# Third modulation group of the even layer summed by VectorE instead of TensorE, with the row handoff to DRAM issued later

## The reference, cut to what matters

```python
mod = jax.nn.silu(c) @ w_ada[layer] + b_ada[layer]
sh1, sc1, g1, sh2, sc2, g2 = jnp.split(mod[:, None, :], 6, axis=-1)
hcur = rms_norm(x, norm1_g[layer]) * (1 + sc1) + sh1
...                      # layer 0: dilated attention (o_a) and spatial gating (o_b)
mix = jnp.concatenate([o_a, o_b], -1) @ ev_w_out[j]
x = x + g1 * mix
hcur = rms_norm(x, norm2_g[layer]) * (1 + sc2) + sh2
x = x + g2 * hierarchical_moe(hcur, ...)
```

## Time and profile before

| | |
|---|---|
| median of 3 runs | 1177.52 us (1177.3 to 1179.76) |
| the profiled execution's own time | 1178.81 us |
| its span on the core | 1177.1 us |
| TensorE matmuls busy | 1114.5 us (95%) |
| VectorE, ScalarE, GpSimd busy | 414.2, 272.4, 91.5 us |
| bytes moved by DMA | 353.83 MB, 301 GB/s in the mean |
| mean granted TensorE clock | 0.989 of full |

### The profile page before, as it was taken

How to read it: one execution, slowest core, us unless ns; L and a number is a source line. 1 busy time by engine, 2 the same in 40 slices (tenths; PEclk the granted TensorE clock), 3 DMA queues, 4 the chain that set the end, 5 groups by cost and what they waited for, 6 DMA issues and landing times.

```text
span 1177.1 us, 17038 instructions
## 1 busy us (share of the span) xinstructions
PE 1114.5 (95%) x6890; PEld 646.3 (55%) x6891; DVE 414.2 (35%) x1065; ACT 272.4 (23%) x579; POOL 91.5 (8%) x156
## 2 busy tenths in 40 slices
PE   3999989999999999989899999998999999999997
PEld 0756434444444378554344444444886878767883
DVE  0275254112111089943511111114541444341213
ACT  2214332111111031162211111114002555541201
POOL 0300030000000000230000000000010323210000
PEclk9999999999999999999899999998999999999999
DMA  9998899999999987995799999999595455344000
GB/s 363 365 355 344 213 417 376 424 425 429 428 428 428 411 325 297 293 274 181 317 379 425 428 429 429 429 430 387 174 291 176 150 167 174 104 149 155 18 1 36
DMA packets 69380, 353.83 MB, mean 301 GB/s; under 512 B 5540, under 2 KB 7756, under 8 KB 49868
## 3 DMA queue, kind: packets, MB, share of 16 engines
q1 hardware_dynamic: 61656, 340.68, 75.1%
q0 software_dynamic: 6000, 9.17, 2.9%
q10 hardware_dynamic: 1668, 3.21, 0.7%
HBM read 350.84 MB, written 1.15 MB: 299 GB/s over the span
## 4 chain that ended last, share of the span: by engine, by line
PE 77%; DMA 15%; DVE 4%; ACT 2%; issue 2%; ACTq 0%; SPq 0%; DVEq 0%
PE bank L497 29%; PE bank L870 22%; DMA ring<-in_moe_w_up 11%; PE bank L535 8%; PE bank L826 3%; PE bank L891 3%; DMA arena<-in_ev_w_s 2%; DVE arena L1738 2%; DMA ring<-in_ev_w_in 2%; PE bank L550 1%; PE bank L1145 1%; PE bank L521 1%; PE bank L509 1%; PE bank L711 1%; PE bank L726 1%
## 5 line engine op out<-in xcount | busy, mean ns | idle before, releaser
L870 PE MATMUL bank<-ring,arena 128*32 128x512 f32 x3072 | 337.5, 595 | 9.7 <-issue 3.9
L497 PE MATMUL bank<-arena,ring 128*128 128x256 f32 x1536 | 340.0, 382 | 1.9 <-ACT arena L1286 1.7
L497 PEld LDWEIGHTS bank<-arena,ring 128*128 128x128 f32 x1536 | 290.5, 191 | 47.3 <-issue 8.7
L870 PEld LDWEIGHTS bank<-ring,arena 128*32 128x32 f32 x3072 | 102.3, 110 | 231.5 <-issue 229.7
L535 PE MATMUL bank<-ring,arena 128*128 128x512 f32 x288 | 126.0, 593 | 0.0
L535 PEld LDWEIGHTS bank<-ring,arena 128*128 128x128 f32 x288 | 54.2, 190 | 65.2 <-issue 64.8
L2258 DVE TENSOR_TENSOR arena<-arena,bank 128x512 f32<-128x512 f32 x16 | 11.0, 687 | 197.0 <-PE bank L870 197.0
L826 PEld LDWEIGHTS bank<-arena 128*128 128x128 f32 x512 | 58.5, 192 | 12.0 <-issue 11.7
L826 PE MATMUL bank<-arena 128*128 128x128 f32 x512 | 61.2, 278 | 0.0
L1464 ACT ACTIVATE arena<-bank 128x512 f32<-128x512 f32 x16 | 9.6, 597 | 210.5 <-PE bank L870 210.5
L891 PE MATMUL bank<-arena 128*128 128x512 f32 x128 | 57.7, 594 | 0.0
(11 more groups left out here) (327 smaller groups left out, 900.6 us busy)
## 6 DMA issues: line engine op xcount, KB each, us to landing
ring<-in_moe_w_gate SPq DMA_DIRECT2D x32, 2048.0 KB, 14.7
ring<-in_moe_w_up SPq DMA_DIRECT2D x32, 2048.0 KB, 17.2
ring<-in_moe_w_down SPq DMA_DIRECT2D x32, 2048.0 KB, 13.0
ring<-in_w_ada SPq DMA_DIRECT2D x24, 2048.0 KB, 21.7
ring<-in_w_in SPq DMA_DIRECT2D x16, 2048.0 KB, 11.2
ring<-in_w_c SPq DMA_DIRECT2D x6, 2048.0 KB, 32.8
ring<-in_ev_w_in SPq DMA_DIRECT2D x5, 2048.0 KB, 14.5
ring<-in_od_w_in SPq DMA_DIRECT2D x5, 2048.0 KB, 15.5
```

The lines of the kernel that those rows point to most:

```text
L497: mm = pe.matmul(ps[k0][:, t * S:(t + 1) * S], w[:, k, c:c + P], rhs[:, k, :], start=(k == 0), stop=(k == KT - 1))
L870: mm = pe.matmul(bank[col:col + CHUNK, :], lhs[:, k, col:col + CHUNK], ring[:, (s0 + e) % RING, cut], start=start, stop=stop, tile_positio ...
```

## The change

Units `ada8` to `ada11` move from TensorE's `group_main` to VectorE's `modulate`: `modulate(8)` stands between `score_max` and `score_probs` of head 4, `modulate(9)`, `(10)` and `(11)` behind `gating()`. Because the sum buffer is reused, the first unit of a later group waits until TensorE has summed the group before. `group_whole(2, 11)` stands between `evo0` and `evo1`, the columns between the two halves of `evo1`. On VectorE `group_cols(2)` and `gain(1)` move behind the two additions of `evo0`; on ScalarE the gate's diagonals (`early_diagonals("gateB")`) move ahead of the third square. On GpSimd's queue the bias table now comes first, behind a wait for the third group's `group_whole`, and `affine_by_row(0)` behind `rpb_sent`. The rest is renamed semaphores: `group_whole` is one counter, and six of the router's become `routing_sums_full` and `routed`.

```diff
-SUMMED = (4, 5, 6, 7, 16, 17, 18, 19, 28, 29)
-SUMMED_GROUPS = (1, 4)
+SUMMED = (4, 5, 6, 7, 8, 9, 10, 11, 16, 17, 18, 19, 28, 29)
+SUMMED_GROUPS = (1, 2, 4)
...
                     if n < 2:
                         quarter_by_channel("ev3", hT, n + 2)
-                    else:
-                        group_main(2, (0, 1))
                 elif n == 0:
                     mix()
-                    group_main(2, (2,))
-                elif n == 1:
-                    group_main(2, (3,))
-                else:
-                    group_columns(2)
...
             by_token("evo0", oT, arrived=heads_out)
-            by_token("evo1", oT, arrived=first_tile(1))
+            group_whole(2, 11)
+            by_token("evo1", oT, lambda: group_columns(2), arrived=first_tile(1))
...
-                if p == 3:
-                    group_copy(2)
                 dilated_out(p)
...
             act.wait_ge(sem("gmlp_ready"), 2)
-            early_diagonals("gateB")
-            routed_norm(1)
+            group_copy(2)
+            routed_norm(1, lambda: early_diagonals("gateB"))
...
+                if n % 4 == 0 and n > 4:
+                    dve.wait_ge(sem("group_whole"), SUMMED_GROUPS.index(n // 4))
...
                 score_max("dilated")
+                if h == 4:
+                    modulate(8)
                 score_probs("dilated")
             gating()
-            group_cols(2)
-            gain(1)
+            for n in (9, 10, 11):
+                modulate(n)
...
                 for b in range(TT):
                     add_mixed(names[0], 0, b, tmp)
+                behind_first()
...
+            def second_group():
+                group_cols(2)
+                gain(1)
+
+            routed_norm(1, ("evo0", "evo1"), second_group)
...
             broadcast_gate(0, mod[:, 16:24])
-            affine_by_row(0)
-            pool.wait_ge(sem("ada_ready"), 12)
+            pool.wait_ge(sem("group_whole"), 2)
             step(pool.memset(rpb_pad[0:16, :, :], 0.0))
...
             pool.wait_ge(sem("rpb_sent"), 16)
+            affine_by_row(0)
```

More of the change, by code:

```diff
@@ L562, in group_whole @@
                                    part[:, 512 * g:512 * g + 512], start=True, stop=True, tile_position=(0, 32 * g))
-                mm.then_inc(sem(f"group_{group}_whole"), 1)
+                mm.then_inc(sem("group_whole"), 1)
             one_of_32 = ident.rearrange("p (g r) -> p r g", r=32)[:, 0, :]
@@ L1350, in group_copy @@
                 if group in SUMMED_GROUPS:
-                    act.wait_ge(sem(f"group_{group}_whole"), 1)
+                    act.wait_ge(sem("group_whole"), SUMMED_GROUPS.index(group) + 1)
                 else:
@@ L1545, in _, with routed_norm @@
                     both("ev3", uT, ACT.Gelu_apprx_tanh)
-            def routed_norm(r):
+            def routed_norm(r, ahead=lambda: None):
                 no = r - 1
@@ L1551, in routed_norm @@
                 for n, (t, h) in enumerate(((0, 0), (1, 0), (0, 1))):
+                    if n == 2:
+                        ahead()
                     act.wait_ge(sem("x_half"), 4 * no + n + 1)
@@ L2082, in route @@
                 lg = rt[:, 0:40].rearrange("p (t c) -> p t c", c=20)
[L2083 to L2085 removed]
+                dve.wait_ge(sem("routing_sums_full"), 3 * layer + 1)
+                dve.tensor_copy(logit_parts, ps[4][:, 0:S]).then_inc(sem("routed"), 1)
+                dve.wait_ge(sem("routing_sums_full"), 3 * layer + 2)
                 dve.wait_ge(sem("rw_loaded"), 16 * 7 * (layer + 1))
@@ L2200, in route @@
                 step(dve.tensor_tensor(by_tile(within), by_tile(rank), slots_bc, ALU.is_le))
-                dve.tensor_tensor(by_tile(over), by_tile(rank), slots_bc, ALU.is_gt).then_inc(sem("over_ready"), 1)
+                dve.tensor_tensor(by_tile(over), by_tile(rank), slots_bc, ALU.is_gt).then_inc(sem("routed"), 1)
                 step.wait()
@@ L2204, in route @@
                 step.wait()
-                dve.wait_ge(sem("over_ready"), layer + 1)
+                dve.wait_ge(sem("routed"), 4 * layer + 4)
                 return weights
@@ L2462, in _ @@
             dve.wait_ge(sem("gate_rows_loaded"), 16)
-            routed_norm(1, ("evo0", "evo1"))
+            def second_group():
+                group_cols(2)
+                gain(1)
+            routed_norm(1, ("evo0", "evo1"), second_group)
             dve.wait_ge(sem("rpb_sent"), 16)
```

18 lines of the change are left out of this document (9 added, 9 removed).

## The result

The changed kernel takes 1196.55 us in the median (1195.85 to 1196.72, 5 runs), the kernel before 1177.52 us on the same chip (1177.26 to 1184.33, 5 runs). The ratio, worked out over all these runs, is 1.0154, with a 95% interval of 1.012 to 1.0189: slower, clear of the noise, though by less than 2%. Between the medians it is 19.0 us. The forecast was 1195.6 us.

The account below looks back on a forecast made before the run. TensorE (77% of the chain) was taken as the bound, counted at the router's start: 17.15 us late plus 1.0 for the clock, +18.1 on 1178.81 is 1196.9. Less 1.3 to the median: 1195.6 us, range 1185 to 1201.

Parts of the forecast that it names:

- the handoff's 22 us from gain to values: GpSimd's queue carries gains and shifts through DRAM to ScalarE's second norm: 22 us, with 3.5 us to spare.
- TensorE's part: From heads to output projection: 8.3 us of matmuls removed, projection starts at 127.6, only 0.4 us left at its end.
- The unit in the gap: `modulate(8)` at head 4 on VectorE waits for TensorE's sum, runs 101.3 to 104.95; loss rounded to 0.5 us.
- GpSimd's queue: Bias table takes 13.4 us, element writes behind it from 156.1 take 14.7, the read 6.3: values at 177.7.
- Rival (1): GpSimd's table gets through before the gain is ready: router +5.2 to +7.5 us, 1183 to 1190 us; chance 0.20.
- The clock's term: Behind TensorE's stand, turns and router's matmuls may run at half speed: nothing to 3.1 us, taken as 1.0.
- Writes that take longer (2): Element writes on GpSimd's queue take 26.7 us: router +25.5 us, 1204 us, half way 1200; chance 0.10.
- Hidden (3): Gain to ScalarE's values within 9.1 us costs nothing: router 0.4 us earlier, 1177.1 us median; chance 0.05.
- Absorbed by the experts' loop (4): The experts' partly DMA-bound loop catches up a few us of the late start: 1188 to 1193 us; chance 0.03.

Follow-up runs that it names:

- e2: Kernel before, with only the bias table moved ahead of the gains and shifts on GpSimd's queue: 1189.12 us, ratio 1.008.
- e3: Changed kernel, layer 0's second norm taking its gains and shifts in their old order without waiting, their four DRAM transfers still running: 1267.35 us.
- e4: Kernel before, with the same edit as e3 (old order, no wait, transfers still running): 1262.84 us.
- e8: e3 with the four transfers of gains and shifts left out altogether: 1265.08 us, ratio 1.0711.
- e11: Changed kernel, with TensorE putting layer 0's second-norm gains and shifts in their second order, nothing through DRAM for them: 1185.51 us, ratio 1.0073.
- e12: Kernel before, with the same edit as e11 (order made by TensorE, no transfers): 1185.12 us, ratio 1.0061.
- e1: Changed kernel, with gains and shifts put ahead of the bias table again on GpSimd's queue: 1194.85 us, ratio 1.0137.
- e5: Changed kernel, with `modulate(8)` moved from head 4 to behind the gating, so four units follow it: 1205.04 us, ratio 1.0205.
- e6: e1 with the shifts sent early on their own behind the gate row, only the gains written late: 1191.53 us, ratio 1.0087.
- e7: e6 with `modulate(9)` ahead of the gating, and `group_whole`, columns and gain moved earlier: 1183.23 us, ratio 1.0036.
- e9: e7 with the bias table made near the start, in bytes free then: 1184.5 us, ratio 1.0055.

## Why the prediction was right, step by step

*The mechanism held.* The step that decided, the handoff's 22 us from gain to values with 3.5 us to spare, is shown from three sides: made late by itself it costs 9 to 12 us (e2); without its wait the routers of both kernels start within 0.3 us of each other (e3, e4), or 1.7 us with the transfers gone too (e8 against e4); and without it altogether the kernels' times differ by 0.4 us (e11, e12). Two later takings bear out the other half, that ScalarE could take the values as late as 160.1: 14.5 us later moved the router by 12.0 us (e2), 19.7 us later by 17.2 us (the kernel after), so 2.5 us beyond the 3.5 cost nothing.

*TensorE's part.* The forecast left 0.4 us of the 8.3 us removed at the projection's end, at 160.1; it ended at 161.7, 1.2 us later than before. The projection was to start at 127.6 and started at 130.12. Of these 2.5 us, 1.0 was there when `mix` started (124.08; 0.9 of it already at the second group's `group_whole`, 101.09 instead of 100.23). The other 1.5 us come behind that, and they are a term that was missing. The forecast let TensorE wait for ScalarE ahead of `mix`, with nothing left to fill the wait, but took `mix` at its old 1.95 us. It took 3.38, and the turn behind it 0.81 instead of 0.55. Ahead of it TensorE had stood for 1.04 and 1.95 us; in the kernel before it was busy throughout, and the granted clock in this window was 1.00. The window of the kernel after:

```profile
124.00:128.00 4.00, 3.92 (x19) 3.65 (x19) 1.95 (x5) 0.24 (x1) 0.55 (x1) 0.57 0.56 37
```

The unit in the gap was released by TensorE's sum as forecast: VectorE's first pass started at 102.33, after `group_whole` at 101.09. `group_whole` of the third group found its three units summed (no stand at 144.03), as forecast too, and the gain was ready at 153.4 instead of 151.0.

*GpSimd's queue.* The bias table's share was right: 13.4 us forecast from `group_whole`'s end to `rpb_sent`, 13.2 measured from the clearing to the writes. The mis-sized term is the writes: 14.7 us were taken from the earlier trace rows, 11.2 were measured; the read's 6.3 us were 7.1. The start 2.3 us late and the writes 3.5 us short cancel but for the read: values at 177.3 (forecast 177.7), router at 183.22 (forecast 183.2). The agreement of the sum is better than that of its terms, and to that extent it is luck.

*What the argument got wrong without harm.* It laid 5 us of the loss on the table standing ahead of the writes. e1 shows 0.4 us at the router: writes that start earlier ran beside more of the ring's loads and lasted longer. Rival (1), less traffic, was so half right: the writes did get shorter, but the table was not through before the gain. The clock's term was 1.0 us. The turn alone took 0.85 us more (1.94 against 1.09), and from the router's first matmul to the experts 20.28 us passed instead of 17.52, 0.77 of it in the router's matmuls; by the end of the span these 2.8 us are gone again, in stretches that the change does not touch. So 17.0 us stand between the profiled executions, where the forecast had 18.1.

*The other rivals.* Writes that take longer (2): the slower one landed after 10.0 us, not 26.7; e2 shows that the direction was possible (17.5 us for the pair), but not in this place. Hidden (3): the writes of the kernel after never landed in less than 8.4 us, and from gain to values it took 24 us where 9.1 would have cost nothing. The Trainium skill, page DMA: Bandwidth & Descriptors (Anatomy of one DMA — SWDGE (gpsimd) path), gives about 2.0 us of fixed cost. No write of single elements in this case comes near it (8.4 us is the shortest in layer 0), and the measurement decides. Absorbed by the experts' loop (4): 19.93 us late at its first matmuls and 20.03 us behind it, at the second layer's first turn, so it absorbed nothing.

*What the trace of before could not show.* The element writes take something from the ring's loads when these are the experts' first weights (e3 against e8: 2.3 us between the medians, 3.2 us from the router to the end). The prediction had the traffic act on the writes, not the writes on the traffic.

## What to carry to other kernels

When work moves to another engine, follow its result to its last reader, through every queue on the way; here 8.3 us taken off the busiest engine weighed nothing against a 22 us handoff that had 3.5 us to spare. Ask of a handoff which spare time it has, before anything ahead of it is made later. A length read beside one traffic is not that beside another: take a range, and when terms agree in the sum, check them one by one. And a filler that is taken out of a busy engine's waits leaves the waits behind, and behind them, here, a lower clock.

## What the runs showed of the hardware

Writing 1024 single values of 4 bytes from 128 partitions to DRAM took, from the first issue to the next instruction behind the last, 11.2 to 12.5 us for a pair of such writes beside 142 GB/s or less (11.7 us with only 23 GB/s and a DMA share of 0.42, in e5), and 14.7 to 17.5 us beside 200 to 218 GB/s. One write alone, beside 224 to 257 GB/s, took 12.7, 14.8 and 13.2 us (e6, e7, e9): halving the values saved a few us at most. From ScalarE's queue the pair took 12.5 us. While they run, loads of 2 MB move slowly in one stretch (57 GB/s at a DMA share of 0.99, against 432 GB/s a few us later), though over the whole of e1's writes they made 200 GB/s; and the instructions that issue loads take longer (5.3 to 6.5 us for two instead of 2.05).

The granted clock fell with TensorE busy all the time by the profile, in the windows around and behind the 32 matmuls with one moving column that e12 adds (112.46 to 114.54). Windows of e12, then of the kernel before at the same place of the program:

```profile
112.00:116.00 4.00, 4.00 (x41) 3.70 (x41) 3.21 (x9) 0.51 (x1) 0.87 (x1) 0.82 0.92 338
116.00:120.00 4.00, 4.00 (x17) 3.33 (x16) 1.36 (x8) 0.80 (x2) 0.03 (x1) 0.76 0.18 12
```

```profile
112.00:116.00 4.00, 4.00 (x22) 3.51 (x21) 3.03 (x13) 1.28 (x3) 0.91 (x1) 1.00 0.34 81
116.00:120.00 4.00, 4.00 (x26) 2.87 (x28) 2.55 (x14) 0.99 (x3) 0.00 (x0) 1.00 0.00 0
```

The sixteen matmuls behind them took 5.41 us in e12 and 3.72 in e11, where the same 32 stand at the same place and the window has 1.00. Behind the second 32, the third group's, both kernels lost 1.7 us: ten matmuls of the projection took 6.26 us in e11 (4.54 in the kernel after), with a granted clock of 0.63 from 156 to 160 us. So the fall is not sure at every such place, and what decides it these runs do not fix. The stand of e5 at the second layer, 3.8 us of it with nothing that the profile shows, is the other open point.
